# Last down weights in raw places of their own, the first gated ahead, value weights split ahead of the norm, cumulative columns behind q: four edits to the third layer of an fp32 network kernel

## What is computed

```python
h = modulate(rms_norm_2(x, norm1_w), sh1, sc1)
p = h @ w_in
...
x = x + g1 * (jnp.concatenate([attn, y_ssd], axis=-1) @ w_out)
x = x + g2 * conv_glu(modulate(rms_norm_2(x, norm2_w), sh2, sc2), ffn_w_up, ffn_conv_w, ffn_conv_b, ffn_w_down)
...
def conv_glu(h, w_up, conv_w, conv_b, w_down):
    gate, val = jnp.split(h @ w_up, 2, axis=-1)
    gate = depthwise_conv(gate, conv_w, conv_b)
    return (jax.nn.silu(gate) * val) @ w_down
```

## Time and profile before

| | |
|---|---|
| median of 3 runs | 1039.73 us (1038.01 to 1039.94) |
| profiled execution, its own time | 1036.11 us |
| its span | 1033.9 us |
| PE busy | 1000.6 us, 97% |
| PE's weight loads | 869.9 us, 84% |
| DVE busy | 696.0 us, 67% |
| ACT busy | 512.7 us, 50% |
| POOL busy | 42.2 us, 4% |
| mean granted clock | 0.997 |
| read from HBM | 180.64 MB |

### The profile page before, as it was taken

One profiled execution on the slowest core, in us unless ns is written; L12 is line 12 of the kernel. 1 busy time (PEld: TensorE's weight loads), 2 busy tenths in 40 slices (PEclk: granted clock), 3 DMA queues, 4 the chain that ended last, 5 costly groups with the idle time before them and its releaser, 6 DMA issues. The chain is left out here.

```text
span 1033.9 us, 15248 instructions
## 1 busy us (share of the span) xinstructions
PE 1000.6 (97%) x6040; PEld 869.9 (84%) x6040; DVE 696.0 (67%) x980; ACT 512.7 (50%) x687; POOL 42.2 (4%) x52
## 2 busy tenths in 40 slices
PE   7999999999989999999999999999999989999996
PEld 5577899999978877899998978979876778999995
DVE  5676657777874576657778572456677677777774
ACT  2366565445554665545445452553444354444443
POOL 0220000000000200000000000000000000000000
PEclk9999999999999999999999999999999999999999
DMA  9035576767645533658886623233101335555532
GB/s 361 14 118 133 204 279 244 249 238 269 255 167 167 198 123 108 266 199 329 334 338 254 248 83 122 82 122 123 41 1 42 129 140 187 189 187 189 190 113 80
DMA packets 29726, 183.92 MB, mean 178 GB/s; under 512 B 3440, under 2 KB 6128, under 8 KB 10096
## 3 DMA queue, kind: packets, MB, share of 16 engines
q1 hardware_dynamic: 25360, 157.56, 42.6%
q0 software_dynamic: 3456, 25.17, 6.3%
q10 hardware_dynamic: 864, 0.55, 0.2%
HBM read 180.64 MB, written 2.62 MB: 177 GB/s over the span
## 5 line engine op out<-in xcount | busy, mean ns | idle before, releaser
L1891 DVE TENSOR_TENSOR split<-raw,split 128x2048 fp32r<-128x2048 f32 (+1 forms) x123 | 279.9, 2276 | 205.9 <-ACT split L1364 205.8
L1364 ACT ACTIVATE split<-raw 128x2048 fp32r<-128x2048 f32 x122 | 231.7, 1899 | 247.3 <-PE bank L671 247.3
L669 PE MATMUL bank<-acts,split 128*128 128x256 f32 (+1 forms) x1024 | 291.0, 284 | 1.8 <-DVE acts L1931 1.4
L671 PE MATMUL bank<-acts,split 128*128 128x256 f32 (+1 forms) x1024 | 290.1, 283 | 0.0
L670 PE MATMUL bank<-acts,split 128*128 128x256 f32 (+1 forms) x1024 | 290.1, 283 | 0.0
L669 PE MATMUL bank<-split,acts 128*128 128x512 f32 (+1 forms) x544 | 211.7, 389 | 1.9 <-DVE split L1891 1.8
L670 PE MATMUL bank<-split,acts 128*128 128x512 f32 (+1 forms) x544 | 209.6, 385 | 0.0
L671 PE MATMUL bank<-split,acts 128*128 128x512 f32 (+1 forms) x544 | 209.2, 385 | 0.0
L669 PEld LDWEIGHTS bank<-acts,split 128*128 128x128 f32 (+1 forms) x1024 | 194.9, 190 | 5.3 <-issue 1.6
L670 PEld LDWEIGHTS bank<-acts,split 128*128 128x128 f32 (+1 forms) x1024 | 195.0, 190 | 2.3
L671 PEld LDWEIGHTS bank<-acts,split 128*128 128x128 f32 (+1 forms) x1024 | 195.0, 190 | 0.4
(11 more groups left out here) (248 smaller groups left out, 1088.1 us busy)
## 6 DMA issues: line engine op xcount, KB each, us to landing
raw<-w_mlp SPq DMA_DIRECT2D x64, 1024.0 KB, 4.8
raw<-w_glu SPq DMA_DIRECT2D x22, 1024.0 KB, 4.7
bias<-w_ada POOLq DMA_DIRECT2D x14, 1024.0 KB, 5.9
raw<-w_qkv SPq DMA_DIRECT2D x12, 1024.0 KB, 4.7
arena<-w_glu_down SPq DMA_DIRECT2D x22, 512.0 KB, 3.2
work<-w_ada POOLq DMA_DIRECT2D x10, 1024.0 KB, 6.1
raw<-w_mla_o SPq DMA_DIRECT2D x4, 1024.0 KB, 5.6
raw<-w_moba_o SPq DMA_DIRECT2D x4, 1024.0 KB, 4.9
```

Of the source, the lines that this page charges most:

```text
L669: pe.matmul(out_, a[0], b[0], start=first, stop=False)
L671: return pe.matmul(out_, a[1], b[0], start=False, stop=last)
L1364: return act.activation(out_, in_, ACT.Copy)
L1891: v.tensor_tensor(split[:, c % 2, 1, 0:n], raw[:, c % 2, 0:n], split[:, c % 2, 0, 0:n].bitcast(F32), ALU.subtract).then_inc(lo_ready, 1)
```

## The change

Four edits, all in the third layer.
- Down weights 20 and 21, the last two, get raw places of their own in `arena` (columns 6144 and 7168) and semaphores of their own. SP issues their loads right behind that of number 18 and ahead of number 19, without a wait. DVE multiplies number 20 by the gate in step 19 and number 21 in step 20. ACT rounds number 21 between the Silu and the split of the product of step 21, instead of behind it.
- The path of down weight 0 stands ahead of step 0: DVE's multiplication between the scaling of the first tile and the modulation, ACT's rounding ahead of step 0's centre tap, DVE's subtraction ahead of its outer taps.
- ACT splits the second chunk of the value weights ahead of its scaling of the second tile and of `gate_out(3)`.
- PE makes the cumulative columns behind the whole of q. ACT splits the second z chunk ahead of the two Exps.

```diff
@@ -315,7 +315,11 @@
         final = arena[:, 8192:8192 + D]
-        raw_down = view(arena, 4096, 2, D)
+        def raw_down(d):
+            at = {KF2 - 2: 6144, KF2 - 1: 7168}.get(d, 4096 + D * (d % 2))
+            return arena[:, at:at + D]
         def split_down(d):
@@ -357,7 +361,7 @@
         out_hi, hidden_hi, glu_taps = sem("head_out_hi_ready"), sem("hidden_hi_ready"), sem("glu_outer_taps")
-        down_loaded = [sem(f"glu_down_loaded{i}") for i in range(2)]
+        down_loaded = [sem(f"glu_down_loaded{i}") for i in range(4)]
         down_gated = sem("glu_down_gated")
@@ -569,11 +573,11 @@
             def load_down(step, i=None):
-                if i is not None or step >= 2:
+                if i is not None or 2 <= step < KF2 - 2:
                     sp.wait_ge(down_lo, step - 1 if i is None else 4 * i + (step - 1))
                 w = weights["glu_down"]
-                sp.dma_start(raw_down[:, step % 2, :], w[step] if i is None else w[4 * i + step])\
-                    .then_inc(down_loaded[step % 2], 16)
+                sp.dma_start(raw_down(step if i is None else step % 2), w[step] if i is None else w[4 * i + step])\
+                    .then_inc(down_loaded[step % 2 + 2 * (i is None and step >= KF2 - 2)], 16)
@@ -586,7 +590,7 @@
             load("glu", 21)
-            for step in range(18, KF2):
+            for step in (18, 20, 21, 19):
                 load_down(step)
@@ -1163,7 +1167,8 @@
             cumulative()
-            rows_units(GC["q"], GU["q"], 4, 512, 512, both[:2], 2, between=cumulative_columns)
+            rows_units(GC["q"], GU["q"], 4, 512, 512, both[:2], 2)
+            cumulative_columns()
             pe.wait_ge(conv_act, 8)
@@ -1671,9 +1676,9 @@
             x_squares(SU["d1"], range(4), True)
+            used(GC["mlp1"] + 31)
             norm_second_tile(14)
             gate_out(3)
-            used(GC["mlp1"] + 31)
             modulated_hi("hx")
@@ -1707,12 +1712,12 @@
             used(GC["q"])
+            used(GC["q"] + 1)
             small_gone(act, SU["cumcol"])
...
             act.activation(tmp(7), sbank(u)[:, 0:64], ACT.Exp).then_inc(small_free[u % 4], 1)
-            used(GC["q"] + 1)
             for n, dst in enumerate((xsr[:, 0], xsr[:, 1], cxsr[:, 0], cxsr[:, 1])):
@@ -1792,6 +1797,16 @@
+            def down_weights(d, i=None):
+                k = 0 if i is None else i
+                act.wait_ge(down_gated, 4 * k + d + 1)
+                if 1 <= d < KF2 - 2:
+                    act.wait_ge(glu_used, 4 * k + d)
+                copy(split_down(d if i is None else 0)[:, 0, :], raw_down(d if i is None else d % 2)).then_inc(down_hi, 1)
+            down_weights(0)
             def glu(s, i=None):
@@ -1805,18 +1820,12 @@
                 act.activation(gact[:, b, :], gact[:, b, :], ACT.Silu).then_inc(glu_act, 1)
+                if s == KF2 - 1:
+                    down_weights(s)
                 act.wait_ge(gemm_free[u % 4], u // 4 + 1 + k)
                 copy(acts[:, 1, 0, T * (s % 4):T * (s % 4) + T], prod_t[:, b, :]).then_inc(hidden_hi, 1)
-                if 1 <= s < KF2 - 1:
+                if 2 <= s < KF2 - 1:
                     down_weights(s - 1, i)
-            def down_weights(d, i=None):
-                k = 0 if i is None else i
-                act.wait_ge(down_gated, 4 * k + d + 1)
-                if 1 <= d < KF2 - 2:
-                    act.wait_ge(glu_used, 4 * k + d)
-                copy(split_down(d if i is None else 0)[:, 0, :], raw_down[:, d % 2, :]).then_inc(down_hi, 1)
@@ -1825,7 +1834,6 @@
                 glu(s)
-            down_weights(KF2 - 1)
             for t in range(2):
@@ -2672,10 +2680,28 @@
                 add_units(GU["out"], (n,), gate=0)
+            def down_low(d, i=None):
+                k, w = 0 if i is None else i, split_down(d if i is None else 0)
+                v.wait_ge(down_hi, 4 * k + (d + 1))
+                v.tensor_tensor(w[:, 1, :], raw_down(d if i is None else d % 2), w[:, 0, :].bitcast(F32), ALU.subtract)\
+                    .then_inc(down_lo, 1)
+            def gate_down(s, i=None):
+                k, w = 0 if i is None else i, raw_down(s if i is None else s % 2)
+                if i is None and s >= KF2 - 2:
+                    v.wait_ge(down_loaded[2 + s % 2], 16)
+                else:
+                    v.wait_ge(down_loaded[s % 2], 32 * k + 16 * (s // 2 + 1))
+                v.tensor_tensor(w, w, gates[:, 1, :], ALU.mult).then_inc(down_gated, 1)
             norm_x(5)
+            gate_down(0)
             modulated_lo("m2", adac[:, 56:64], adac[:, 16:24])
...
             used(GC["out"] + 3)
+            down_low(0)
@@ -2702,21 +2728,14 @@
                                 acts[:, 1, 0, T * (s % 4):T * (s % 4) + T].bitcast(F32), ALU.subtract).then_inc(act_lo, 1)
-                if 1 <= s < KF2 - 1:
+                if 2 <= s < KF2 - 1:
                     down_low(s - 1, i)
-                gate_down(s, i)
-            def down_low(d, i=None):
-                k, w = 0 if i is None else i, split_down(d if i is None else 0)
-                v.wait_ge(down_hi, 4 * k + (d + 1))
-                v.tensor_tensor(w[:, 1, :], raw_down[:, d % 2, :], w[:, 0, :].bitcast(F32), ALU.subtract).then_inc(down_lo, 1)
-            def gate_down(s, i=None):
-                b, k = s % 2, 0 if i is None else i
-                v.wait_ge(down_loaded[b], 32 * k + 16 * (s // 2 + 1))
-                v.tensor_tensor(raw_down[:, b, :], raw_down[:, b, :], gates[:, 1, :], ALU.mult).then_inc(down_gated, 1)
+                if 1 <= s < KF2 - 2:
+                    gate_down(s, i)
+                if s == KF2 - 3:
+                    gate_down(s + 1)
+                if s == KF2 - 2:
+                    gate_down(s + 1)
```

## The result

The kernel after takes **1029.57 us** in the median of four runs (1028.80 to 1030.34), the one before 1039.74 in these rounds; the medians are 10.2 us apart, where 6.3 were forecast. The ratio on record, with its 95% interval, is 0.9914 (0.9900 to 0.9929); it is an estimate of its own and not the quotient of the medians (0.9902), and the interval reaches from 7.4 to 10.4 us. The profiled execution of after took 1030.01 us with a span of 1027.7 us. The forecast for these two was 1029.8 and 1027.6. So the profile moved as forecast, to 0.2 us, and the medians moved by 3.9 us more. The experiments are about that difference.

The account below looks back on a forecast made before the run. PE, busy 97% of the span, was taken as the bound, with four stalls to cut: -1.3 - 0.8 - 2.3 - 1.9 = -6.3 us, from the 1039.73 median to 1033.4 us, range 1030.8 to 1036.8.

Parts of the forecast that it names:

- Value weights: Stall of 1.77 us before the value product: ACT's earlier split lets PE go on 1.3 us sooner, 0.4 stays.
- Cumulative columns: q stage: PE's wait before the columns goes, a new stall of 0.94 for ACT's Exp comes; -0.8 us.
- First down weights: Stall of 2.11 us before the first down product goes, with inputs ready early; -2.3 us, bounds -2.3 and -1.1.
- the hole: DVE's idle 1.16 us before the modulation, to take the 1.22 us gate multiplication, at most 0.05 late.
- Last down weights: Stall of 1.76 us before the last down product goes altogether; -1.9 us, bounds -1.7 and -2.0.
- the 0.21 left: PE's wait of 0.21 us before 1019.16 stays, since the subtraction it waits for does not move.
- the hole held the multiplication: Rival: the gate multiplication does not fit DVE's idle time before the modulation; gain 5.1, 1034.6 us; chance 0.08.
- the table switch costs its load: Rival: ACT's table switch before the Exp costs more than its load; gain 5.1, 1034.6 us; chance 0.05.
- the loop has no wait at step 1: Rival: the gated loop takes gain back, step 1's down product waits; gain 4.0, 1035.7 us; chance 0.07.
- the first load was there in time: Rival: first down weights land late, every gated-stage product waits; slower than before, 1042 us or more; chance 0.02.
- The granted clock is 1.00 around the longest of them: Clock at its upper level, 2.4 GHz, around the 2.11 us stall; such stalls cost only their own length.
- It lies 3.6 below the median of the three runs shown: Forecast profiled time, 1029.8 us, from 1036.11 profiled; the offset to the 1039.73 median is carried over, giving 1033.4.

Follow-up runs that it names:

- a_again: The kernel after, unchanged, run again beside before: 1029.64 us against 1037.67, ratio 0.9922.
- value_only: Before with only the value weights' split moved ahead of the norm's second-tile scaling: 1038.08 us against 1037.50, ratio 1.0000.
- undo_cols: The kernel after with the cumulative columns back between the halves of q: 1033.76 us; before 1038.14, ratio to before 0.9943.

## Why the prediction was wrong

The direction and each of the four steps were right, the size was not, and the range (1030.8 to 1036.8) missed the result by 1.2 us.

- **Value weights.** Forecast -1.3 with 0.4 of the stall left; -1.32 and 0.47 in the trace. Right as a step; alone it is worth nothing in the median, which nothing in the prediction had foreseen.
- **Cumulative columns.** Forecast -0.8 with a new stall of 0.94 for the Exp; -0.97 with 0.54. The mechanism was right. ACT's chain was summed 0.15 too long, at its two ends. The rest of the 0.40 is no error of the chain: the forecast counts from where PE could go on, the profile's idle figure from a modelled end 0.25 later (692.86 less 690.82 less 1.25 is 0.79).
- **First down weights.** Forecast -2.3, at most 0.05 late in the hole; -2.3, not late. **Last down weights.** Forecast -1.9 with the 0.21 left; -1.9 and 0.21.
- The rivals did not happen: the hole held the multiplication, the table switch costs its load, the loop has no wait at step 1, the first load was there in time (slowest landing 7.6 us).
- **The step that failed** is the sentence in the first part: "The granted clock is 1.00 around the longest of them ... so stalls of this length cost their own length and nothing more". It was read from one execution, around one stall, and the clock behind a given stall differs from execution to execution. The same trace spoke against it: behind the 1.70 us at 305.69 the clock is at 0.50 from 308 to 310. Three places have such falls: before's own two profiles show those in the first MLP's end and behind the columns' stall, and profiles of kernels that keep before's lines show the one before the first down product. The change takes the stall away at two of them. In the sum a term is missing: the mean clock of before is 0.9957, 0.9956 and 0.9952 in its three groups of rounds, that of a_again 0.9973. 0.0016 to 0.0017 of 1031 us is 1.7 us, about one fall for each run, whose price between two traces was 1.6. By that 6.5 becomes 8.1 or 8.2; 8.0 was measured side by side.
- The rest, 2.1 us, is the level of before. **"It lies 3.6 below the median of the three runs shown; the difference is carried over"** took an offset for constant that was itself made, in part, of falls that the change removes and, in part, of three high runs out of a wide scatter (65 runs on three chips, with a median of 1037.8). The clocks of those three runs are not on record, so how the offset divides is an estimate. It was the clue: 3.6 us that the trace did not contain is time that no row of this trace can explain, and the range should have reached down by as much.

What stays open: what decides in which execution the clock falls. The stall of 1.77 before the value product (six profiles), the one of 1.76 before the last down product (six) and the two of 1.5 and 1.4 around the last norm (all fourteen) are about as long, and no trace here shows a fall behind them. So the length of a stall alone does not decide, and no run separates it from the work around it: the columns' stall is followed by sixteen small matmuls, which after has too, but with no stall ahead. The scale does not close either: the runs of before at 0.994 or less are in the median 2.1 us longer than those at 0.997, where two falls would make 3.2. Why value_only has more falls behind a stall that it does not touch was not tried further.

## What to carry to other kernels

Look at the clock and the span of every run beside the one that is profiled: two levels of span that go with two levels of the granted clock mean that some stall costs more than its length in part of the runs, and one trace can show such a place as harmless. Look through the profiled run itself for low windows too, and not only around the stalls that the change touches. Price a stall of PE at its length plus its share of falls (here 1.6 to 1.7 us for each, twice that for a long one), and measure an edit alone and in company: value_only took away 1.3 us of a stall and gained nothing, because its runs had more falls elsewhere. Where the profiled execution lies clearly off the median, put that offset into the range, not only into the middle.

## What the runs showed of the hardware that was not expected

- Behind the same 1.57 us stall of one kernel the granted clock stayed at 2.4 GHz in one execution and was at 1.2 GHz from about 687.3 to 690.6 us in another; with the stall at the same place undo_cols had it low for the whole of 687 to 693, sixteen products in 6 us. In these two traces the fall starts after PE has begun to work again, not within the stall. At the first down product of value_only it starts before: the mean from 855.50 to 855.98 is 0.79, and the product starts at 855.98.
- Levels other than 0.50 and 1.00 appear only in windows that hold a change of level. The Trainium skill ("TensorE: Matmul & The Clock Gate", Part 1: The HAM clock gate) describes a gate that passes either half or all of the pulses by how busy PE has been. The windows here agree as to the two levels.
- A table load of ACT took 1.28 us, and the Exp behind it started 0.01 later.
- A DVE multiplication of 1.22 us fitted into a hole of 1.16: it started 0.09 before the end of the scaling ahead of it (828.88, 828.97), and the modulation started 0.03 after its end, with no delay against the stage ahead.
